# One stationary for w and the decayed q of a chunk in a gated delta-rule layer

## What is computed

```python
u = jnp.einsum('bhnij,bhnjd->bhnid', tmat, vb)
w = jnp.einsum('bhnij,bhnjd->bhnid', tmat, kb * jnp.exp(gc)[..., None])
attn = jnp.einsum('bhnik,bhnjk->bhnij', q, k) * decay
qg = q * jnp.exp(gc)[..., None]
kg = k * jnp.exp(gc[..., -1:] - gc)[..., None]

def step(S, inp):                      # one chunk after the other
    qg_c, kg_c, u_c, w_c, attn_c, gl_c = inp
    v_new = u_c - w_c @ S
    o = qg_c @ S + attn_c @ v_new
    S = S * gl_c + kg_c.T @ v_new
    return S, o

o = rmsnorm(o, g_norm) * silu(z)
```

## Time and profile before

| | us |
|---|---|
| median of 3 runs | 4400.4 (4399.14 to 4402.82) |
| the profiled execution | 4404.4 |
| its span in the profile | 4402.6 |
| TensorE matmuls busy in the span | 4049.9 (92%) |
| VectorE, ScalarE, GpSimd busy | 1967.2 (45%), 1414.8 (32%), 780.5 (18%) |
| stores of `oa`, first and last | 2212.1, 3070.5 |

### The profile page before, as it was taken

The page is one execution under the profiler, slowest core; times in us unless marked ns, Lnnn a source line. Parts: engine busy times, 40 slices in busy tenths (PEclk is TensorE's granted clock), DMA queues, the critical chain, the costliest instruction groups (busy, mean ns, idle before and its releaser), DMA issues. The chain is left out here.

```text
span 4402.6 us, 57342 instructions
## 1 busy us (share of the span) xinstructions
PE 4049.9 (92%) x22955; PEld 2618.4 (59%) x22955; DVE 1967.2 (45%) x4330; ACT 1414.8 (32%) x2972; POOL 780.5 (18%) x544
## 2 busy tenths in 40 slices
PE   8999999998899999997999999996999989899877
PEld 4555555554455554544888888885666565565544
DVE  0111111111333333333466655553157676778875
ACT  2222222222111111111333333331245454555553
POOL 1323323223022222221122222221000000000000
PEclk9999999998999999998999999995999999999998
DMA  5000000002201111114000000002100100000000
GB/s 185 20 18 10 19 14 14 19 14 110 90 30 35 35 35 35 35 35 148 21 26 25 21 25 25 21 21 83 67 22 30 34 18 22 29 17 18 17 13 17
DMA packets 89739, 162.43 MB, mean 37 GB/s; under 512 B 17381, under 2 KB 49466, under 8 KB 89402
## 3 DMA queue, kind: packets, MB, share of 16 engines
q1 hardware_dynamic: 89530, 159.53, 10.6%
HBM read 120.18 MB, written 39.33 MB: 36 GB/s over the span
## 5 line engine op out<-in xcount | busy, mean ns | idle before, releaser
L349 PE MATMUL e_ps<-arena,e_xT 128*128 128x440 f32 (+1 forms) x1792 | 689.3, 538 | 2.7 <-DMA arena<-l_w_in 2.7
L863 PE MATMUL o_ps<-arena,o_xT 128*128 128x512 f32 x1280 | 564.5, 594 | 0.8 <-ACT o_xT L971 0.8
L349 PEld LDWEIGHTS e_ps<-arena,e_xT 128*128 128x128 f32 x1792 | 333.4, 191 | 304.6 <-issue 296.5
L863 PEld LDWEIGHTS o_ps<-arena,o_xT 128*128 128x128 f32 x1280 | 239.2, 191 | 279.1 <-issue 279.0
L1393 PE MATMUL d_ps<-hT_in,arena 128*128 128x128 f32 x3072 | 392.2, 282 | 13.3 <-ACT hT_in L1579 11.3
L1393 PEld LDWEIGHTS d_ps<-hT_in,arena 128*128 128x128 f32 x3072 | 359.4, 193 | 29.0 <-ACT hT_in L1579 12.6
L2183 PE MATMUL s_ps<-hT_in,arena 128*128 128x128 f32 x2160 | 257.3, 279 | 7.0 <-PEq L67 7.0
L2183 PEld LDWEIGHTS s_ps<-hT_in,arena 128*128 128x128 f32 x2160 | 253.6, 196 | 10.4 <-issue 9.4
L952 PE MATMUL o_ps<-o_w_out,o_gt 128*128 128x512 f32 x512 | 225.2, 598 | 4.6 <-ACT o_gt L1028 4.6
L2307 PE MATMUL s_ps<-arena 128*128 128x512 f32 x512 | 228.4, 600 | 0.0
L446 PE MATMUL e_ps<-e_w_out,e_gt 128*128 128x512 f32 x512 | 224.1, 596 | 0.0
(11 more groups left out here) (416 smaller groups left out, 6162.0 us busy)
## 6 DMA issues: line engine op xcount, KB each, us to landing
xb<-x SPq DMA_DIRECT2D x64, 512.0 KB, 3.4
o_scratch<-w_ada SPq DMA_DIRECT2D x16, 768.0 KB
arena<-l_w_in SPq DMA_DIRECT2D x5, 2048.0 KB, 18.3
arena<-w_in SPq DMA_DIRECT2D x5, 2048.0 KB, 13.4
x<-e_gl SPq DMA_DIRECT2D x16, 512.0 KB
x<-o_cat SPq DMA_DIRECT2D x16, 512.0 KB
hT<-hT_in SPq DMA_DIRECT2D x16, 512.0 KB, 2.6
out<-xb SPq DMA_DIRECT2D x16, 512.0 KB, 2.9
```

The lines of the kernel that those rows point to most:

```text
L349: m = pe.matmul(bank[c % 2][:, 0:n], xT[:, k * P:(k + 1) * P], W_in[:, k, a:a + n], start=(k == 0), stop=(k == KT - 1))
L863: m = pe.matmul(bank[c % 2][:], xT[:, k * P:(k + 1) * P], W_in[:, k, off:off + 512], start=(k == 0), stop=(k == KT - 1))
```

## The change

w and the decayed q of a chunk share one tile, `wq` of [128, chunk, head, 128]. For chunk 0 the first 64 columns are w and the last 64 the decayed q; for chunk 1 it is the other way round. One product with S (128 columns of stationary) thus gives both wS and qS: in bank 7 for chunk 0, with wS on partitions 0 to 63 and qS on 64 to 127, and in bank 2 for chunk 1, with qS on 0 to 63 and wS on 64 to 127. So wS stands where u has its rows, and o stands with its chunks swapped and in two banks: chunk 0 on partitions 64 to 127 of bank 7, chunk 1 on 0 to 63 of bank 2.

What follows from that: the attention products write to the other half of the partitions; the square of o, and `oa`, are made in two halves with half the partitions each (two squares for one, eight `oa` instructions for four); z is copied with its halves swapped, so that the gate fits (four copies of 64 partitions and one of b, a for two copies); `oa` is stored by two DMAs, swapped back; the decayed q is made in two halves. On TensorE, one fill is added between the merged product and the products with `kg` of chunk 0, and the three fills behind `turn_qk` become two. The wait for the previous block's `oa` is moved ahead of the five rounds, since bank 2 now holds part of o.

```diff
--- before.py
+++ after.py
@@ -1255,7 +1255,6 @@
         vb = sb("vb", [P, 4, P])
         qT = sb("qT", [P, 4, P])
         kT = sb("kT", [P, 4, P])
-        qgT = qn
         L = sb("L", [P, 4, DC])
         Lm = sb("Lm", [P, 4, DC])
         Lm2 = sb("Lm2", [P, 4, DC])
@@ -1263,7 +1262,7 @@
         R = sb("R", [P, 4, DC])
         X = sb("X", [P, 4, DC])
         attn = sb("attn", [P, 4, DC])
-        wT = sb("wT", [P, 4, P])
+        wq = sb("wq", [P, 2, 4, P])
         u = sb("u", [P, 4, P])
         vnew = sb("vnew", [P, 4, P])
         S = sb("S", [P, 4, P])
@@ -1354,10 +1353,11 @@
                     sp.wait_ge(*hs_ready.upto(b.i + 3))
                     sp.dma_start(xb[:, b.q, :], x[bass.ds(b.i * P + 5 * P, P), :]).then_inc(x_in[b.q].sem, 16)
                 sp.wait_ge(*oa_ready.upto(b.i))
-                sp.dma_start(oa_out[bass.ds(b.i * P, P), :], oa[:]).then_inc(oa_stored.sem, 16)
+                for a in (0, DC):
+                    sp.dma_start(oa_out[bass.ds(b.i * P + a, DC), :], oa[DC - a:P - a, :]).then_inc(oa_stored.sem, 16)
 
             over_pipeline(sp, body)
-            sp.wait_ge(oa_stored.sem, 16 * BLOCKS + 1)
+            sp.wait_ge(oa_stored.sem, 32 * BLOCKS + 1)
             sp.wait_ge(h_stored.sem, 16 * BLOCKS + 1)
 
         @block.tensor
@@ -1479,6 +1479,8 @@
                 if not b.last2:
                     turn_h(b.i + 2)
                 pe.wait_ge(*R_ready.upto(i))
+
+                pe.wait_ge(*oa_ready.before(i))
                 for s in range(5):
                     pe.wait_ge(*Lm_ready.upto(i, s + 1))
                     if s:
@@ -1514,18 +1516,16 @@
                 pe.wait_ge(*u_ready.upto(i))
                 pe.wait_ge(*qg_ready.upto(i))
 
-                pe.wait_ge(*oa_ready.before(i))
                 for n in range(2):
                     a = 64 * n
                     if n:
                         pe.wait_ge(*S_ready.upto(i, 1))
                     for h in range(4):
-                        m = pe.matmul(bank[2][a:a + 64, h * P:(h + 1) * P], wT[:, h, a:a + 64], S[:, h, :], start=True, stop=True)
+                        m = pe.matmul(bank[(7, 2)[n]][:, h * P:(h + 1) * P], wq[:, n, h, :], S[:, h, :],
+                                      start=(h == 0), stop=False, skip_group_check=True)
                     m.then_inc(*wS_made.inc())
-
-                    for h in range(4):
-                        pe.matmul(bank[7][a:a + 64, h * P:(h + 1) * P], qgT[:, h, a:a + 64], S[:, h, :],
-                                  start=(h == 0), stop=False, skip_group_check=True)
+                    if n == 0:
+                        fill()
                     if n and not b.last:
                         turn_v(j)
                     pe.wait_ge(*vnew_ready.upto(i, n + 1))
@@ -1536,12 +1536,12 @@
                         fill()
                 pe.wait_ge(*attn_ready.upto(i))
                 for h, a in tiles:
-                    m = pe.matmul(bank[7][a:a + DC, h * P:(h + 1) * P], attn[a:a + DC, h, :], vnew[a:a + DC, h, :], start=False,
-                                  stop=True, skip_group_check=True)
+                    m = pe.matmul(bank[2 if a else 7][DC - a:P - a, h * P:(h + 1) * P], attn[a:a + DC, h, :], vnew[a:a + DC, h, :],
+                                  start=False, stop=True, skip_group_check=True)
                 m.then_inc(*o_made.inc())
                 if not b.last:
                     turn_qk(j)
-                    fill(3)
+                    fill(2)
                     turn_normalised(j)
                     key_products(j)
                 fill(17)
@@ -1583,7 +1583,12 @@
                 if c < 3:
                     act.activation(cv[:, p, 4 * c:4 * c + 4, 3:P + 3], by_head[c % 2], ACT.Copy).then_inc(*proj_ready.inc())
                 else:
-                    act.activation(zba[:, p, (c - 3) * ZH:(c - 2) * ZH], bank[c % 2][:, 0:ZH], ACT.Copy).then_inc(*proj_ready.inc())
+                    n = ZH if c == 3 else 512 - ZH
+                    for a in (0, DC):
+                        act.activation(zba[DC - a:P - a, p, (c - 3) * ZH:(c - 3) * ZH + n], bank[c % 2][a:a + DC, 0:n], ACT.Copy)\
+                           .then_inc(*(proj_ready if c == 3 and a else o).inc())
+                    if c == 4:
+                        act.activation(ba[:, p, :], bank[c % 2][:, n:ZH], ACT.Copy).then_inc(*proj_ready.inc())
 
             def softplus(i, p):
 
@@ -1712,8 +1717,8 @@
                         if not b.last2:
                             project(b.i + 2, p, 1)
                 act.wait_ge(*wu_made.upto(i))
-                act.activation(wT[:, :, 0:DC], by_chunk[2], ACT.Copy).then_inc(*wT_ready.inc())
-                act.activation(wT[:, :, DC:P], by_chunk[5], ACT.Copy).then_inc(*wT_ready.inc())
+                act.activation(wq[:, 0, :, 0:DC], by_chunk[2], ACT.Copy).then_inc(*wT_ready.inc())
+                act.activation(wq[:, 1, :, DC:P], by_chunk[5], ACT.Copy).then_inc(*wT_ready.inc())
                 act.activation(u[:], by_head[3], ACT.Copy).then_inc(*u_ready.inc())
                 if not b.last:
                     silu_step(j, 2)
@@ -1721,7 +1726,8 @@
                 if not b.last2:
                     project(b.i + 2, p, 2)
                 act.wait_ge(*o_made.upto(i))
-                act.activation(osq[:], by_head[7], ACT.Square).then_inc(*osq_ready.inc())
+                act.activation(osq[DC:P], by_head[7][DC:P], ACT.Square).then_inc(*o.inc())
+                act.activation(osq[0:DC], by_head[2][0:DC], ACT.Square).then_inc(*osq_ready.inc())
                 if not b.last:
                     square_qk(j)
                 act.wait_ge(*so_ready.upto(i))
@@ -1880,7 +1886,7 @@
                 for n in range(2):
                     a = 64 * n
                     dve.wait_ge(*wS_made.upto(i, n + 1))
-                    dve.tensor_tensor(vnew[a:a + 64], u[a:a + 64], by_head[2][a:a + 64], ALU.subtract).then_inc(*vnew_ready.inc())
+                    dve.tensor_tensor(vnew[a:a + 64], u[a:a + 64], by_head[(7, 2)[n]][a:a + 64], ALU.subtract).then_inc(*vnew_ready.inc())
                     if not b.last:
                         (silu, weigh_v)[n](j)
                     dve.wait_ge(*U_made.upto(i, n + 1))
@@ -1896,10 +1902,12 @@
                 dve.wait_ge(*ro_ready.upto(i))
                 dve.wait_ge(*gz_ready.upto(i))
 
-                dve.wait_ge(oa_stored.sem, 16 * i + 1)
-                for h in range(4):
-                    dve.scalar_tensor_tensor(oa[:, h * P:(h + 1) * P], by_head[7][:, h, :], ro[:, h:h + 1], gz[:, h, :],
-                                             ALU.mult, ALU.mult).then_inc(*(oa_ready if h == 3 else o).inc())
+                dve.wait_ge(oa_stored.sem, 32 * i + 1)
+                for n, a in ((7, DC), (2, 0)):
+                    for h in range(4):
+                        dve.scalar_tensor_tensor(oa[a:a + DC, h * P:(h + 1) * P], by_head[n][a:a + DC, h, :], ro[a:a + DC, h:h + 1],
+                                                 gz[a:a + DC, h, :], ALU.mult, ALU.mult)\
+                           .then_inc(*(oa_ready if n == 2 and h == 3 else o).inc())
                 if not b.last:
                     for stage in (normalise_qk, copy_kT, mask_products):
                         stage(j)
@@ -1929,7 +1937,8 @@
             def decay_q(i):
 
                 pool.wait_ge(*qT_ready.upto(i))
-                pool.tensor_tensor(qgT[:], qT[:], eG[:], ALU.mult).then_inc(*qg_ready.inc())
+                pool.tensor_tensor(wq[:, 0, :, DC:P], qT[:, :, 0:DC], eG[:, :, 0:DC], ALU.mult).then_inc(*o.inc())
+                pool.tensor_tensor(wq[:, 1, :, 0:DC], qT[:, :, DC:P], eG[:, :, DC:P], ALU.mult).then_inc(*qg_ready.inc())
 
             shift_h(0)
             shift_h(1)
```

## The result

The changed kernel takes 4440.5 us (median of 4 runs, 4437.5 to 4442.7) against 4400.3, a ratio of 1.009 with a 95% interval of 1.0073 to 1.0108. The forecast was 4441 and slower, with a range of 4416 to 4460.

What follows compares the result with a forecast made beforehand. TensorE sets the pace, with an equally long ScalarE/VectorE chain before the transposes. Fourteen blocks lose 1.39 (19.5) plus 1.5 for the clock (21), the end 0: 40.5 us, median 4441, range 4416 to 4460.

Steps and rivals of the forecast that it cites:

- The bound: From turn_qk to the transposes, TensorE's pieces and the ScalarE/VectorE chain to qn end together; neither has slack.
- The merged product: wS and qS products in one: 8 records take 0.99 us, 0.94 less per chunk, 1.88 a block.
- Chunk 0 and 1: Block start to turn_qk: chunk 0 ends at 5.77 us, chunk 1 waits for vnew, turn_qk begins at 9.88.
- The road behind `turn_qk`: turn_qk to transposes: 5.97 plus 0.06 (second square) plus 1.04 (four more oa) gives 7.07 us; transposes 1.39 later.
- The clock: TensorE's 2.5 to 2.8 us gap before the transposes makes its clock fall to half, costing 1.5 us a block.
- How the price of the clock arises: Half rate costs 1.54 us from transposes to L; the cover during T nearly holds; 1.5 taken.
- Edits at nothing: Longer z, b, a copies 0 to 0.1 us, halved decay_q 0.1 to 0.3, second store 0.3 of issue; all covered.
- the signs at the end of the prediction: oa store spacing: 60 us if right, 58.6 if the clock step was wrong, 55.3 if the bound was misread.
- No fall of the clock: Rival: the stall before the transposes passes at 2.4 GHz, only 19.5 us lost, 4420; chance 0.14.
- TensorE stays the bound: Rival: each block gains 1.88 us, 4374, if the turn_qk-to-transposes chain is at most 4.2 us; faster 0.05.
- Dearer: Rival: attention pairs don't overlap (4454) or falls cost 2.5 us a block (4455); 0.11 together with no saving.
- without saving: Rival: a merged product takes 1.9 us, so nothing is saved, about 4467; 0.11 together with the dearer case.

Runs made afterwards that it cites:

- e4: The kernel before with only its four oa instructions made into eight of half the partitions; 4410.4 us, ratio 1.0026.
- e5: The kernel before with its four oa instructions moved behind normalise_qk on VectorE; 4390.8 us, ratio 0.9981.
- e8: The changed kernel with five useless matmuls on TensorE where it waits for qn, in the fourteen blocks with pieces; 4420.9 us, ratio 1.0045.
- e1: The changed kernel with its eight oa instructions moved on VectorE, four behind normalise_qk and four behind the copy of kT; 4397.6 us, ratio 0.9998.
- e3: The changed kernel with ten useless matmuls on TensorE where it waits for qn, in the fourteen blocks with pieces; 4413.8 us, ratio 1.0034.
- e6: The changed kernel with the oa instructions moved, no fill in chunk 0 and three fills behind turn_qk again; 4392.5 us, ratio 0.9981.
- e2: The changed kernel with the fill put back: none in chunk 0, three behind turn_qk; 4401.3 us, ratio 1.0008.

## Why the prediction was right, point by point

- *The bound.* Right: two roads of nearly one length. e4 lengthens VectorE's by 1.32 and the block grows by 1.14; e5 shortens it and the loop stays. That neither had slack was read from the weight loads: `qn` ends at 2617.00, the first load follows at 2617.08, but the first matmul only at 2617.30. So VectorE's road had some 0.2 to spare.
- *The merged product.* Right. Eight records take 0.9 to 1.0 us (2624.10 to 2625.00, where the next piece starts). The rule by which nothing would be saved doesn't hold for this stream.
- *Chunk 0 and 1.* 5.72 and 4.01 against 5.77 and 4.11; the wait for `vnew` in chunk 1 is there (0.42). `turn_qk` comes at 9.73 and not 9.88. The attention products still overlap: they begin at 2632.81, and `turn_qk` follows 1.02 behind.
- *The road behind `turn_qk`.* Forecast 7.07, measured 7.35. VectorE's chain grew by 1.40 (5.89 to 7.29, to the end of `qn`) where I had 1.10. Both terms were sized too small. The second square begins 0.62 behind the first and not 0.48, so that the squares of q and k start 0.10 later and not 0.06, and eight `oa` instructions take 2.32, so 1.20 more and not 1.04. A third term, 0.12, I hadn't named: the first `oa` instruction no longer overlaps the sum before it. Two other errors cancel this: `turn_qk` comes 0.15 earlier than forecast, and the slack of 0.2 is used up first. So the transposes come 1.30 later against 1.39 forecast, and the block at the full clock is 1.24 longer.
- *The clock.* The fall in all fourteen blocks was right, and its price, 1.66 against 1.5. Drawing the line by the length of the gap is refuted: behind gaps of 1.6 us (e8), 1.2 (e1) and even 0.9 (e4) some blocks have a fall. At 2.7 it made no difference. The falls of the trace before were also read too narrowly: most last 3.4 to 10 us, but four last 13.7 to 23.9 and one 64.9, between the layers and in the last two blocks.
- *How the price of the clock arises.* That it came out near is in part luck. I had read 1.54 from the transposes to `L`, and nothing behind that. In the block shown the clock falls 1.1 us after the transposes have begun, so that it costs only 0.8 up to `L` (3.97 against 3.15 in e3). The cover behind `L` doesn't hold: the last piece ends too late for `T` (2647.95), whose product starts at 2648.72, and `turn_h` waits for the z copies; from `L` to `turn_h` it is 4.80 against 3.47, 1.3 more. That makes 2.1 in a block with 6.8 us at half rate, and the mean is near 1.5 because four of thirteen have 3.4 and lose 0.84.
- *Edits at nothing.* The copies of z, b, a were one waiter short. I looked at `add_dt_bias` and the copy of R; `turn_h` of the next block also waits for them, 0.4 in most blocks. It does so only behind a fall, so it is inside the 1.66. The distance of the stores, given as 57.2, was misread; it is 57.6 (and TensorE's busy time in the earlier trace rows is 54.7, not 54.5). The sum doesn't use it, but the signs at the end of the prediction do: its 58.6, 60 and 55.3 should each be 0.4 more.
- *The sum.* 13 x 2.90 = 37.7, 1.2 for the first block's own part and 2.0 for the fall of the clock in the fourteenth, 6.8 us long and behind its store: 40.9, where 40.5 was forecast for fourteen. But the whole came out right partly by luck. Of the 38.3 us of span, 2.7 more arise up to the first store, most of it where the half rate ahead of the first block lasts twice as long (6.8 and not 3.4). From the fourteenth store to the sparse layer it is 5.0 more; less the 2.0, some 3.0 are left for the last two blocks, where I had 0 ± 2. And the untouched sparse layer gives 8.3 back. The last blocks are a term that I had mis-sized, and why wasn't looked into; the other two I hadn't named.
- *The rivals.* "No fall of the clock" is e3, 4414. "TensorE stays the bound" fails at the point named: the other road is 7.35 and not under 4.2. "Dearer" and "without saving" didn't happen.

## What to carry to other kernels

A list that is busy because fill work stands in its waits has no slack to give away. Before taking a piece of cover from a place, measure the chain that it covers; if both end together, what is added to the chain is paid almost in full (1.14 of 1.32 us in e4). A layout that halves partitions doubles the instructions of every elementwise step that reads it, and what counts is whether one of those steps stands on such a chain. When a new wait of TensorE appears, price the clock behind it as well: here it cost more than the wait's own excess over the old road.

## What the runs showed of the hardware

- **The clock's falls reach unchanged code.** The sparse layer is the same in every kernel here, with the same 6194 matmul records, but takes 1320 to 1329 us, and the more of it falls at the half rate, the longer it is. It was 95 us at half rate in the changed kernel, 117 in the kernel before and 120 in e6 (1329 us too); the four kernels in which the layer takes 1324 to 1325 us have 107 to 113. These are rows by stretch of that layer, of the changed kernel:

```profile
3120.40:4440.90 1320.50, 1164.32 (x6194) 767.16 (x6194) 889.15 (x1649) 641.01 (x1327) 65.13 (x48) 0.96 0.08 27
```

  and of the kernel before:

```profile
3073.80:4402.60 1328.80, 1175.32 (x6194) 774.49 (x6194) 890.17 (x1649) 639.55 (x1327) 65.15 (x48) 0.96 0.08 26
```

  (Rounded, the clock is 0.96 in both.) So a total that moves by less than 0.2% may say nothing of the edit; the distance of a recurring event inside the loop does. Why the falls come out differently wasn't settled.
- **The length of a gap isn't all.** Gaps of 1.6 us at the end of the even layer's blocks are never followed by a fall. The same length with gaps of 0.8 and 1.0 close behind it is, in six of fourteen blocks (e8), and 1.2 us in eight of fourteen (e1). A gap of 0.92 is in two of fourteen (e4) and one of 0.99 in one (e2). What decides between blocks is open.
- **A change of partitions costs the overlap.** Two squares on all partitions take 1.08 in the kernel before. On two different halves the second starts only when the first has ended (0.59 long, 0.62 apart). On VectorE, eight `oa` instructions in two partition halves take twice what four take, without the overlap that I had counted on between the halves: the fifth starts 0.40 behind the fourth (0.37 long), where neighbours of one half start 0.26 apart. The Trainium skill, "VectorE: DVE Perf Modes", section "Two Vector instructions with no wait between them", gives a model by which an instruction whose input or output starts in another quadrant (32 partitions) than the last one's is held until all earlier ones have finished. The rows of VectorE agree, and those of ScalarE show the like.
- **A tenth of a microsecond behind a piece.** The merged product follows a projection piece 1.89 us after that piece's start; the 64-column product followed at 1.98. The Trainium skill, "TensorEngine Tiling (Array Packing)", section "Key Properties", says that a change of tiling mode drains the TensorE. A tenth of a microsecond at this place would fit that, but the products with `kg`, which have 64 rows, also start only 1.88 behind a piece in the changed kernel (2625.00 to 2626.88). No run here isolates it, and the cause stays open.
